# Biased softmax attention of the first network: the values of one task and the turn of the next stand together

## What is computed

```
s = jnp.einsum('bqhd,bkhd->bhqk', q_i, k_i).astype(jnp.float32) + bias[None]
s = jnp.where(valid[None, None, None, :], s, NEG_INF)
p = jax.nn.softmax(s, axis=-1).astype(v.dtype)
return jnp.einsum('bhqk,bkhd->bqhd', p, v_i)
```

## Time and profile before

| | |
|---|---|
| median of 3 runs | 1985.35 us (1984.89 to 1985.43) |
| the profiled execution | 1985.54 us |
| its span, first to last instruction | 1983.7 us |
| PE busy | 1971.5 us (99%) |
| DVE busy | 1246.3 us (63%) |
| ACT busy | 911.0 us (46%) |
| POOL busy | 99.7 us (5%) |
| mean granted clock of TensorE | 0.999 |

### The profile page before, as it was taken

One profiled execution on the slowest core, in us unless ns is written; L12 is line 12 of the kernel. 1 busy time (PEld: TensorE's weight loads), 2 busy tenths in 40 slices (PEclk: granted clock), 3 DMA queues, 4 the chain that ended last, 5 costly groups with the idle time before them and its releaser, 6 DMA issues.

```text
span 1983.7 us, 31862 instructions
## 1 busy us (share of the span) xinstructions
PE 1971.5 (99%) x13856; PEld 1800.7 (91%) x13856; DVE 1246.3 (63%) x1772; ACT 911.0 (46%) x1221; POOL 99.7 (5%) x84
## 2 busy tenths in 40 slices
PE   8999999999999999999999999999999999999998
PEld 7888999999888999999999989899999998989997
DVE  6566666555656766655565567665566556776555
ACT  4445544444445545444444445544444444555442
POOL 0000001000100000100110020010010002001000
PEclk9999999999999999999999999999999999999999
DMA  8544566666554456696666656468666665646663
GB/s 291 174 144 143 178 205 197 198 208 191 172 168 149 140 179 195 196 261 186 175 211 191 188 154 170 111 196 258 191 170 210 187 186 150 177 120 195 185 188 106
DMA packets 421445, 361.85 MB, mean 182 GB/s; under 512 B 29424, under 2 KB 361528, under 8 KB 421304
## 3 DMA queue, kind: packets, MB, share of 16 engines
q1 hardware_dynamic: 421160, 359.74, 60.0%
q10 hardware_dynamic: 144, 0.07, 0.0%
HBM read 358.72 MB, written 1.05 MB: 181 GB/s over the span
## 4 chain that ended last, share of the span: by engine, by line
PE 99%; DVE 0%; DMA 0%; DVEq 0%; ACT 0%; issue 0%
PE ps L217 23%; PE ps L219 23%; PE ps L218 23%; PE ps L224 8%; PE ps L226 8%; PE ps L225 8%; PE ps L1521 3%; PE ps L1632 1%; PE ps L1666 1%; PE ps L1637 0%; PE ps L1704 0%; PE ps L1655 0%; DMA xs<-in_x 0%; PE ps L1772 0%; PE ps L1788 0%; PE ps L1681 0%
## 5 line engine op out<-in xcount | busy, mean ns | idle before, releaser
L2040 DVE TENSOR_TENSOR hl<-raw,hl 128x1024 fp32r<-128x1024 f32 (+2 forms) x535 | 722.5, 1384 | 381.3 <-ACT hl L1816 380.7
L217 PE MATMUL ps<-xt,hl 128*128 128x256 f32 (+1 forms) x2672 | 754.2, 282 | 0.0
L218 PE MATMUL ps<-xt,hl 128*128 128x256 f32 (+1 forms) x2672 | 746.1, 279 | 0.0
L219 PE MATMUL ps<-xt,hl 128*128 128x256 f32 (+1 forms) x2672 | 745.8, 279 | 0.0
L1816 ACT ACTIVATE hl<-raw 128x2048 fp32r<-128x2048 f32 (+1 forms) x338 | 613.9, 1825 | 222.9 <-PE ps L226 162.5
L217 PEld LDWEIGHTS ps<-xt,hl 128*128 128x128 f32 (+1 forms) x2672 | 500.9, 187 | 5.5 <-issue 2.3
L218 PEld LDWEIGHTS ps<-xt,hl 128*128 128x128 f32 (+1 forms) x2672 | 501.0, 188 | 3.2
L219 PEld LDWEIGHTS ps<-xt,hl 128*128 128x128 f32 (+1 forms) x2672 | 500.8, 187 | 0.2
L224 PE MATMUL ps<-hl,o 128*128 128x512 f32 x656 | 261.6, 399 | 0.0
L226 PE MATMUL ps<-hl,o 128*128 128x512 f32 x656 | 259.0, 395 | 0.0
L225 PE MATMUL ps<-hl,o 128*128 128x512 f32 x656 | 258.8, 394 | 0.0
(11 more groups left out here) (197 smaller groups left out, 1576.2 us busy)
## 6 DMA issues: line engine op xcount, KB each, us to landing
raw<-in_w_in SPq DMA_DIRECT2D x83, 1024.0 KB, 5.1
raw<-in_w_ffn_in SPq DMA_DIRECT2D x88, 512.0 KB, 5.2
raw<-in_ffn_gate SPq DMA_DIRECT2D x88, 512.0 KB, 4.0
raw<-in_ffn_up SPq DMA_DIRECT2D x88, 512.0 KB, 5.3
raw<-in_ffn_down SPq DMA_DIRECT2D x44, 1024.0 KB, 5.2
raw<-in_w_ffn_out SPq DMA_DIRECT2D x22, 1024.0 KB, 5.1
raw<-in_w_out SPq DMA_DIRECT2D x24, 512.0 KB, 4.9
raw<-in_w_branch_a SPq DMA_DIRECT2D x8, 1024.0 KB, 5.1
```

Source lines behind the costliest of these rows:

```text
L217: e.matmul(out, l[0], r[0], start=start, stop=False)
L218: e.matmul(out, l[0], r[1], start=False, stop=False)
L219: return e.matmul(out, l[1], r[0], start=False, stop=stop)
L2040: e.tensor_tensor(lo[:, c], m["raw"][:, k % NRAW, 0:n][:, c], hi[:, c].bitcast(F), ALU.subtract).then_inc(s.low.up(("low", k), *([("low", ...
```

## The change

The chunk attention is driven by a new function `joined` in place of `slots`. It takes the same steps in the same order, but yields only twice a round: once after the scale of the last task and the scores of the newest, and once after the values of one task and the turn of the next, with the sum of their costs. A yield is left out when its sum is 0, which also removes the two `PART` yields of the rounds 4 and 5. The differential attention keeps `slots`.

```
+    def joined(tasks):
+
+        for n in range(len(tasks) + 2):
+            for group in ((-1, 0), (-2, -1)):
+                sum_ = 0
+                for x in group:
+                    if 0 <= n + x < len(tasks):
+                        sum_ += next(tasks[n + x])
+                if sum_:
+                    yield sum_
...
-            yield from slots([task(i, jp) for i in range(2) for jp in range(2)], (-1, 0, -2, -1))
+            yield from joined([task(i, jp) for i in range(2) for jp in range(2)])
```

## The result

| | before | changed |
|---|---|---|
| median | 1985.24 us (6 runs, 1984.83 to 1985.43) | 1997.78 us (6 runs, 1996.54 to 1998.61) |
| profiled execution / its span | 1985.54 / 1983.7 us | 1996.84 / 1995.0 us |
| PE busy | 1971.5 us | 1973.7 us |
| DVE busy | 1246.3 us | 1246.5 us |
| mean granted clock | 0.999 | 0.998 |

The account below looks back on a forecast made before the run. It took PE's queue, busy 99% of the span, as the bound. Waits of 10.1 us, less 0.1 saved, plus 2.2 for the clock give 12.2 on 1985.54, less 0.19 for the median: 1997.5 us, range 1994.8 to 2000.3.

Parts of the forecast that it names:

- No wait left that could absorb a new one: Whole kernel: PE's only waits are 5.1 and 0.4 us in the first 10 us, so new waits add in full.
- PE arrives at 155.89 and waits 4.5 us: Layer 0, values of task 2: PE comes at 155.89, DVE's copy to `et` ends at 160.40, a 4.5 us wait.
- The end of DVE's copy is fixed: Chunk attention, task 2: DVE's copy ends at 160.40 behind splits and rotations, however early PE comes.
- The second wait, ahead of the turn of task 3: Turn of task 3 needs the scaled `er`, ready at 162.41, so it ends at 162.84; total delay 5.07 us a layer.
- The waiting without the clock: 10.0 us: Rival, both layers: waits come but the clock holds, 1995.3 us; chance 0.31 for holding in at least one.
- The clock: 2.2 us: After the new wait PE's clock falls to half in both layers, costing 1.1 us each, 2.2 in all.
- Savings of 0.1 us: Values and turn as neighbours save passages to the projection; only the third counts, 0.05 us a layer, 0.1 in both.
- Second chain: Rival: the delay makes a later split or differential attention step late, 1.2 to 2.8 us more; chance 0.08.
- no wait: Rival: DVE reaches the copy of task 2 earlier, only savings remain, 1985.05 us; chance 0.03 for none or nearly none.

Follow-up runs that it names:

- the copies on ACT: The changed kernel with both copies of task 2 made by ACT instead of one by ACT and one by DVE; 1997.85 us, ratio 1.0064.
- the rotations: The changed kernel with the two rotations of k for the differential attention moved on DVE behind the scaling of task 3; 1996.89 us, ratio 1.0060.
- 14 transposes: The changed kernel with 14 identity transposes on PE ahead of the values of task 2, into a bank nobody reads; 1995.04 us, ratio 1.0050.
- the dropped yields: The kernel before the change with only the two yields of rounds 4 and 5 left out, nothing joined; 1997.75 us, ratio 1.0064.
- 38 transposes: The changed kernel with 38 identity transposes on PE ahead of the values of task 2, into a bank nobody reads; 1995.64 us, ratio 1.0053.

## Why the prediction was right

- *No wait left that could absorb a new one.* Right. One layer costs 6.2 us and two 12.5.
- *PE arrives at 155.89 and waits 4.5 us.* 4.63 and 4.62. By distances between starts PE arrives at 155.42 (151.01 plus 0.59, 0.85 and 2.97), the forecast less the 0.47 by which it is ahead there. What the working left out is the passage from the end of the copy to the start of the values: the copy ends at 159.96 and the waiting values start at 160.12, 0.16 later. So of the 0.18 us by which the copy seemed to be early before the change, some 0.02 were real room.
- *The end of DVE's copy is fixed.* Right: the copy starts 0.43 earlier in an execution in which the values of task 1 are 0.47 earlier too. That it is the queue and not the copy is shown by the copies on ACT, and what it stands behind by the rotations.
- *The second wait, ahead of the turn of task 3.* It has gone into the slow values, as worked out. Where the clock holds (14 transposes) it is there: by distances 0.30 (values from 160.29 plus 1.03, turn at 161.62) where 0.37 was taken, and the turn takes 1.01 instead of 0.85 as its last half waits too, 0.16 where 0.18 was taken.
- *The waiting without the clock: 10.0 us.* 9.96 by the kernel with 14 transposes.
- *The clock: 2.2 us.* 2.6 by the medians, and 2.0 in the profiled execution. There, from the start of the values to the end of the turn, it is 3.33 (160.12 to 163.45) against 2.34 (160.29 to 162.63) where the clock holds, 0.99 a layer beside the 1.1 of the prediction. That the size fits is in part luck: 1.1 is the middle between two bounds 1.1 us apart. Of what they were made of, the slow values took 1.90 and not 2.06, and the slow turn 1.43, 1.7 times its 0.85, not 2.3 times as at the kernel's start. And the triples behind the turn, which the middle left out, were slow in some executions.
- *The spread of the runs*, which the prediction doesn't name. The slow stretch has no fixed length: it is 3.4 us long in both layers of this profile, 6.8 and 3.4 in that of the dropped yields, 6.8 twice with both copies on ACT. The mean granted clock of each run of the changed kernel is on record: 0.998 in the two shortest (1996.54 and 1996.84 us), 0.997 in the next (1997.42), 0.996 in the three longest (1998.13 to 1998.61). So the longer ones spent more time at half clock, and the profiled execution is one of the short ones. The runs of the dropped yields are not in that order (1997.54 has 0.996, 1997.96 has 0.998), so the spread is borne out for the changed kernel and not shown in general.
- *Savings of 0.1 us.* Wait and slower steps give 4.63 + 0.87 + 0.58 = 6.08 in layer 0 and 4.62 + 0.87 + 0.62 = 6.11 in layer 1, 12.2 in all. By distances the changed kernel loses 6.04 us from the first scores of layer 0 to those of layer 1 (123.74 and 615.98 before, 123.33 and 621.61 after), and 5.97 more up to a step in the second network (1266.62, and 1278.22 after), 12.0 in all. The 0.2 between are what the six shorter passages can have saved. The profiled executions differ by 11.3 only, since this one was 0.4 ahead before the attention, and 0.3 is gained in the second network, where the change does nothing (the last matmul is 11.29 late); the kernel with the change in layer 0 alone gains there too.
- *Second chain, no wait.* Neither came.

One thing was not in the prediction: it took the change as one, counting the matmuls that were gone between turn and values, and did not say which of the two edits took them away. The experiments show that the neighbourhood costs nothing that can be told from no change (0.7 us more with both yields kept, 0.1 us less with one), and that the one yield of round 4 which fell away with it, 18 matmuls and 4 transposes, costs the 12.5 us.

## What to carry to other kernels

Where the busiest engine shows no waits, look for the steps at which it arrives just after what it needs (here 0.18 us after the end of the copy, of which 0.16 are the passage from a copy to the matmuls that wait for it): these are covered by work that happens to stand there, and a reorder that looks neutral, even one dropped empty slot at the end of a loop, uncovers them in full. Work out the arrival of each engine apart, by distances from start to start, and ask what holds the slower engine's queue. Once the new order leaves PE idle for microseconds, add the stretch at half clock: here 1.0 us a layer in the profiled execution and 1.3 by the medians, on top of a wait of 4.6.

## What the runs showed of the hardware

- The granted clock fell to 0.50 at each of the seven waits of 4.4 to 4.6 us that were profiled (the changed kernel, the dropped yields, both copies on ACT, layer 0 alone). How long after PE's last work it fell differs: 4.4 us in the changed kernel (155.49 to 159.8), 2.5 in layer 0 of the dropped yields (155.52 to 158.0), 2.5 in layer 0 with both copies on ACT (156.52 to 159.0), and in layer 1 of the dropped yields only behind the wait, 0.7 us after PE had started again.
- It also fell 1.8 us into a wait of 2.09, with a wait of 0.66 and 1.0 us of matmuls ahead of it (the rotations later), and held with waits of 1.22 and 1.66 us and 1.75 us of transposes between them (14 transposes), and with one wait of 1.22 and 38 transposes behind it. What decides stays open.
- The slow stretch lasted 3.4 us or 6.8. In it a matmul of 512 columns takes 0.43 us instead of 0.23, the values 1.90 instead of 1.03, and a turn of 8 transposes 1.43 (1.59 with both copies on ACT) instead of 0.85.
- Values that wait for a copy by DVE start 0.16 us after its end (159.96 to 160.12).
